# Bringing each block's gate and up biases by DMA, and adding them with two-row products

## What is computed

```python
logits = (xf @ w_router + b_router)
top_v, top_e = lax.top_k(logits, TOP_K)          # 4 of 32 experts
...
def expert_block(args):
    xe, e = args
    gu = xe @ w_gu[e] + b_gu[e]                  # 1024 -> 2048, gate and up interleaved
    gate = jnp.minimum(gu[..., 0::2], SWIGLU_LIMIT)
    up = jnp.clip(gu[..., 1::2], -SWIGLU_LIMIT, SWIGLU_LIMIT)
    act = (up + 1.0) * (gate * jax.nn.sigmoid(gate * SWIGLU_ALPHA))
    return act @ w_dn[e] + b_dn[e]
```

## Time and profile before

| what | us |
|---|---|
| median of 3 runs | 1533.24 |
| lowest and highest | 1531.03 and 1533.29 |
| the profiled execution's own time | 1530.54 |
| its span, first to last instruction | 1528.2 |

### The profile page before, as it was taken

The page is one execution under the profiler, slowest core; times in us unless marked ns, Lnnn a source line. Parts: engine busy times, 40 slices in busy tenths (PEclk is TensorE's granted clock), DMA queues, the critical chain, the costliest instruction groups (busy, mean ns, idle before and its releaser), DMA issues.

```text
span 1528.2 us, 20819 instructions
## 1 busy us (share of the span) xinstructions
PE 1453.2 (95%) x6962; PEld 1184.8 (78%) x6962; DVE 1304.7 (85%) x1231; ACT 1016.8 (67%) x903; POOL 203.9 (13%) x149
## 2 busy tenths in 40 slices
PE   5999989778999999999999999999999999999994
PEld 5776867666888888888888888888888888888882
DVE  5348554768999999999999999999999999999998
ACT  5334444336777777777777777777777777777771
POOL 0000000021111112211111111112211112111100
PEclk9999999878999999999999999999999999999997
DMA  9311030349999999999999999999999999999994
GB/s 353 113 68 56 33 138 15 120 170 378 360 372 367 361 376 360 371 373 369 377 382 372 376 368 366 362 377 365 371 372 375 378 371 373 379 366 361 366 375 166
DMA packets 98157, 471.77 MB, mean 309 GB/s; under 512 B 12649, under 2 KB 12690, under 8 KB 63826
## 3 DMA queue, kind: packets, MB, share of 16 engines
q1 hardware_dynamic: 87682, 451.72, 75.9%
q0 software_dynamic: 10448, 19.70, 3.6%
HBM read 467.70 MB, written 21.50 MB: 320 GB/s over the span
## 4 chain that ended last, share of the span: by engine, by line
PE 89%; DVE 7%; DMA 1%; issue 1%; ACT 1%; SPq 0%; DVEq 0%; ACTq 0%; POOLq 0%
PE gu_bank L1246 17%; PE gu_bank L1247 17%; PE gu_bank L1248 17%; PE turn_bank L1246 8%; PE turn_bank L1248 8%; PE turn_bank L1247 8%; PE bank L1494 2%; PE bank L1501 2%; DVE w_lo L828 2%; PE bank L1246 2%; PE bank L1248 1%; PE bank L1247 1%; PE gu_bank L1486 1%; PE bank L1418 1%; PE gu_bank L1364 1%
## 5 line engine op out<-in xcount | busy, mean ns | idle before, releaser
L828 DVE TENSOR_TENSOR w_lo<-raw,w_hi 128x2048 fp32r<-128x2048 f32 x411 | 931.9, 2288 | 113.3 <-ACT w_hi L578 107.7
L578 ACT ACTIVATE w_hi<-raw 128x2048 fp32r<-128x2048 f32 x411 | 784.8, 1921 | 231.1 <-PE gu_bank L1248 187.0
L1246 PE MATMUL gu_bank<-w_hi,turned 128*128 128x512 f32 (+1 forms) x1096 | 430.5, 393 | 8.5 <-DVE turned L1129 8.2
L1247 PE MATMUL gu_bank<-w_lo,turned 128*128 128x512 f32 (+1 forms) x1096 | 427.1, 390 | 0.0
L1248 PE MATMUL gu_bank<-w_hi,turned 128*128 128x512 f32 (+1 forms) x1096 | 426.8, 389 | 0.0
L1246 PEld LDWEIGHTS gu_bank<-w_hi,turned 128*128 128x128 f32 x1096 | 207.2, 189 | 51.0 <-issue 7.1
L1248 PEld LDWEIGHTS gu_bank<-w_hi,turned 128*128 128x128 f32 x1096 | 207.2, 189 | 42.8
L1247 PEld LDWEIGHTS gu_bank<-w_lo,turned 128*128 128x128 f32 x1096 | 207.4, 189 | 41.3
L1246 PE MATMUL turn_bank<-w_hi,turned 128*128 128x512 f32 (+1 forms) x544 | 213.4, 392 | 0.0
L1248 PE MATMUL turn_bank<-w_hi,turned 128*128 128x512 f32 (+1 forms) x544 | 210.4, 387 | 0.0
L1247 PE MATMUL turn_bank<-w_lo,turned 128*128 128x512 f32 (+1 forms) x544 | 210.3, 387 | 0.0
(11 more groups left out here) (265 smaller groups left out, 1303.7 us busy)
## 6 DMA issues: line engine op xcount, KB each, us to landing
raw<-in_w_gate_up_dram SPq DMA_DIRECT2D x264, 1024.0 KB, 7.7
raw<-in_w_down_dram SPq DMA_DIRECT2D x132, 1024.0 KB, 9.7
raw<-in_w_in_dram SPq DMA_DIRECT2D x10, 1024.0 KB, 7.7
raw<-in_w_out_dram SPq DMA_DIRECT2D x4, 1024.0 KB, 5.5
raw<-expert_rows SPq DMA_DIRECT2D x4, 1024.0 KB, 6.2
raw<-in_w_mem_kv_dram SPq DMA_DIRECT2D x2, 1024.0 KB, 8.9
arena<-in_x_dram SPq DMA_DIRECT2D x1, 2048.0 KB, 14.6
arena<-in_position_tables_dram SPq DMA_DIRECT2D x1, 2048.0 KB, 19.5
```

Source lines behind the costliest of these rows:

```text
L578: a.activation(home, raw_ap, ACT.Copy).then_inc(hi_ready, 1)
L828: v.tensor_tensor(home[1], raw_ap, home[0].bitcast(F32), ALU.subtract).then_inc(lo_ready, 1)
L1246: pe.matmul(bank, a[0], b[0], start=first, stop=False)
L1247: pe.matmul(bank, a[0], b[1], start=False, stop=False)
```

## The change

All of the split biases are written once from `bias` to a tensor in memory, `split_biases` (512 KB), by Pool. For each block Pool then reads the block's expert's rows back: four transfers of 2 rows (high and low) by 512 numbers, each to two partitions of `bias_now`, at partitions 0, 32, 64 and 96. `gu_bias` adds them with four products of 2 rows by a tile of ones, `ones_r`, one product in each group of 32 partitions, and waits for the four transfers instead of for `pick`. The expert's number is read by Pool (`value_load`) from `exp_i`. DVE makes `ones_r` once and no longer makes `pick`.

```diff
+    bias_dram = nc.dram_tensor("split_biases", (P, FF), F32).ap()
+    bias_rows = bias_dram.rearrange("(g i e) (h n) -> i e h g n", g=2, i=2, h=2)
...
-        pick = R[:, 7 * D:7 * D + P]
+        ones_r = R[:, 7 * D:7 * D + P]
+        bias_now = R[:, 5 * D:5 * D + 512]
...
+            def bias_of(e):
+
+                for c in range(4):
+                    pool.dma_start(bias_now[c * E:c * E + 2, :].unsqueeze(1),
+                                   bias_rows[:, e, c // 2, c % 2, :]).then_inc(bias_now_in, 16)
+
+            pool.wait_ge(bias_ready, 2)
+            pool.dma_start(bias_dram, bias).then_inc(bias_saved, 16)
+            pool.wait_ge(bias_saved, 16)
+            bias_of(slice(0, 1))
             pool.tensor_copy(idx_scatter, y_row_i[:, bass.ds(loops, 1)]).then_inc(idx_ready, 1)
...
+            def bias_of_block(b):
+
+                bias_of(bass.ds(pool.value_load(exp_i[0:1, bass.ds(b, 1)], min_val=0, max_val=E - 1), 1))
+
             with pool.Fori(1, loops) as b:
                 pool.wait_ge(xtp_done, b + 1)
                 gather(bass.ds(b + 1, 1), b * 2 + 1)
+                bias_of_block(b)
                 scatter(b - 1, b * 2 + 2)
+            pool.wait_ge(xtp_done, loops + 1)
+            bias_of_block(loops)
             scatter(loops - 1, loops * 2 + 1)
...
                 link(v.tensor_copy(bias, bias_in))
+                v.tensor_copy(ones_r, ones).then_inc(ones_ready, 1)
...
-            def choose(into, ready, column):
-
-                v.tensor_scalar(into, cst[:, C_ROWMOD:C_ROWMOD + 1].to_broadcast([P, P]), exp_f[:, column], None,
-                                ALU.is_equal).then_inc(ready, 1)
...
-            def gu_bias(n_pick):
-
-                pe.wait_ge(pick_ready, n_pick)
+            def gu_bias(n_in):
+
+                pe.wait_ge(bias_now_in, n_in)
                 for c in range(4):
-                    rows = slice(c % 2 * 2 * E, (c % 2 + 1) * 2 * E)
-                    ins = pe.matmul(psum[c], pick[rows, :], bias[rows, c // 2 * 512:(c // 2 + 1) * 512],
-                                    start=False, stop=True)
+                    rows = slice(c * E, c * E + 2)
+                    ins = pe.matmul(psum[c], ones_r[rows, :], bias_now[rows, :], start=False, stop=True)
                 ins.then_inc(gu_done, 1)
...
-            pe.wait_ge(bias_ready, 2)
-            gu_bias(1)
+            pe.wait_ge(ones_ready, 1)
+            gu_bias(64)
...
-                gu_bias(b + 1)
+                gu_bias(b * 64 + 64)
```

More of the change, by code:

```diff
@@ L289, in hymba_layer @@
         atp_done, ahi_ready, alo_ready = sem("atp_done"), sem("ahi_ready"), sem("alo_ready")
-        pick_ready = sem("pick_ready")
+        ones_ready, bias_saved, bias_now_in = sem("ones_ready"), sem("bias_saved"), sem("bias_now_in")
         map_ready, map_in, map_out, part_in, part_added = (
@@ L1164, in _ @@
             number_blocks()
-            choose(pick, pick_ready, slice(0, 1))
             for i in range(4, GU):
@@ L1171, in _ @@
             clamp(1)
-            choose(pick, pick_ready, slice(1, 2))
             lo_m(GU + 2)
@@ L1186, in _ @@
                 clamp(b + 1)
-                choose(pick, pick_ready, bass.ds(b + 1, 1))
                 lo_m(GU + 11, b)
```

## The result

| | before | after |
|---|---|---|
| median, 5 runs each | 1533.29 us | 1543.09 us |
| lowest and highest | 1531.03 and 1535.58 | 1542.29 and 1545.75 |

The ratio is 1.0067, with a 95% interval of 1.0051 to 1.0083: slower by 9.8 us in the medians. Forecast were 5.7 us. The profiled execution of after took 1545.5 us, with a span of 1543.8.

The account below looks back on a forecast made before the run. The prediction took PE, full in the loop, to bound the kernel. It added 16.4 us at the start and took off 10.7 in the loop, +5.7 on 1533.24, for 1539 us, range 1531 to 1546.

Parts of the forecast that it names:

- What bounds the kernel: In the loop PE is busy 35.00 of 35 us without waits, so a microsecond off PE is one off the time.
- The write behind the loads: Ahead of the loop, the 512 KB write follows Pool's earlier loads in its queue, landing 15.7 us after its issue.
- The four reads: Ahead of the loop, after the write: the fourth read starts 1.5 us later and lands in 3.1, biases there at 363.4.
- The start: Ahead of block 1: PE waits for write and reads, starting at 370.0 instead of 353.67, +16.4 us once.
- the wait for `turn_x`: Sign at the start, between blocks 0 and 1: PE waits again about 6 us for L1129.
- The step saved on PE: Bias products in the loop: one step in place of two saves 0.335 us per block, -10.7 us over 32 blocks.
- The Trainium skill's factor: Bias products in the loop: four row-packed products at 3.07 times one after the other, saving 0.23 a block, 7.4 us in all.
- In the loop, hidden: Pool's reads for block 2 land at 408.2 to 414.0, before PE needs them at 414.58.
- Rival 1: At the start, the write doesn't queue and lands in 4.0 us: sum -6.1, 1527 us; chance 0.10.
- Rival 2: In the loop, biases come late in every block: at 10 us to the landing +15, 1554 us; chance 0.04.
- Rival 3: The four bias products don't run at once, nothing saved: +16.4, 1549.6 us; chance 0.06.

Follow-up runs that it names:

- block 0 the old way: The changed kernel, but block 0's biases are added as in the kernel before, blocks 1 to 32 the new way: 1524.8 us, ratio 0.9952 to the kernel before.

## Why the prediction was right, point by point

The forecast was 1539 us, slower, with 1531 to 1546 as its range; 1543.09 lies in it. The mechanism held, and one term was mis-sized.

- **What bounds the kernel.** Right: PE has no wait in the loop of after, and what was saved per block came off the time, as the kernel with block 0 the old way shows on its own.
- **The write behind the loads.** Right, and nearly to the number: 15.7 us from issue to landing forecast, 15.8 measured, with 3.7 us behind the slowest load where 3.0 were taken. The choice between a bound of 4.0 and one of 17.7 was made by asking what stood ahead of it in the same queue, and moving those loads took 7.1 us off. What this didn't foresee is the rest: even then it needs 8.75.
- **The four reads.** 1.5 us of issue and 3.1 to the last landing forecast, 1.55 and 2.62 measured. The reason given (a small read with nothing ahead of it in its queue) was luck in part: the weight loads had just run dry. A read that met other transfers took 5.36, and in the loop of after the reads take 6.0 at the median.
- **The start.** +16.4 us forecast (its own terms, 370.0 - 353.67, give 16.3), +16.9 measured. The forecast left out the 0.28 us between the end of `split_biases` and the write, as much again before the reads, and 0.14 before the products; the reads' 0.5 less paid for most of it. Of its signs one failed here: the wait for `turn_x` is 4.2 us, not about 6.
- **The step saved on PE.** Too large: 0.335 us a block taken, 0.224 measured, 10.7 against 7.2 us over 32 blocks. This is 3.5 of the 4.1 us by which the forecast was short. The other 0.5 are the start's. The step that failed is the reading of the earlier trace rows: the second pair stands 0.335 behind the first, and I took the distance for the price of a pair. But a lone pair takes 0.43 to the turning of the rows, a lone set of four 0.43 to 0.44, and a second pair or a second set costs 0.21 to 0.24 more. So 0.335 holds a part that the first set pays whatever follows, most likely its own weight load, which finds no product to hide behind (that it is the load wasn't tried by itself); the set taken away was worth about one step of the products around it, 0.23. The row was there: the products of 128 rows start 0.23 apart, and the second pair is at work beside the first's tail.
- **The Trainium skill's factor** ("TensorE: Matmul & The Clock Gate", Part 3, measured speedup: 3.07 for four packed products) gave 7.4 us for this term, an estimate, and the measured 7.2 stands by it rather than by mine. In part this is luck: the factor is for four products one after the other, and it was applied to the step of 0.335, which is not the price of one.
- **In the loop, hidden.** Right: the fourth read was issued at about 426.9 (425.27 + 2.10 less one issue of 0.5) and had until 437.2. The slowest of all reads in the loop landed 7.3 us after its issue, 3 us in time, and leaving the reads out changed nothing.
- **Rival 1** (the write doesn't queue) fell at the landing of 15.8. The Trainium skill ("DMA: Bandwidth & Descriptors", Anatomy of one DMA) gives 2.0 us plus bytes over 436 GB/s, by which this write would take an estimated 3.2 us: the traces don't agree, with 15.8 here, 8.75 without the loads ahead of it, and 4.0 for a write of this size in the quiet stretch. **Rival 2** (late in every block) fell with PE's empty list of waits. **Rival 3** (not at once) fell: four starts within 0.01 us, and 0.22 us a block gained.

## What to carry to other kernels

When data that a loop needs takes a detour through memory, look at its first use by itself: the detour was free for 32 blocks and cost 16.9 us for the one that had no work in front of it, and keeping the old path for that one block turned 10 us lost into 8 us gained. Before you price a transfer, ask what was issued on the same queue just before, and what else keeps the DMA engines busy: here the first was worth 7.1 of 15.8 us, and the write without it still took 8.75 against 4.0 in a quiet stretch. The distance between the starts of the first two members of a short series is not the price of a member: take it from a run with one member more or less (0.21 to 0.24 us here), or from the distance in steady flow (0.23).

## What the runs showed of the hardware that was not expected

- A set of products in different partition groups takes 0.43 us from its first product to the next products when it stands alone between products of 128 rows, whether it is two of 64 rows or four of 2 rows, and 0.21 to 0.24 for each further set.
- A read of 4 KB issued by Pool took 2.62 us where the weight loads had just run dry, 5.36 where weights and other loads of Pool were moving, and 6.0 at the median in the loop.
- The granted clock between 200 and 250 us was 0.97 in some traces and 0.86 in others, with nothing in that part changed. Each kernel has one trace, but the kernel before alone had a mean granted clock of 0.978 at about 1530.7 us and of 0.972 at about 1535.7: about 5 us of the time.
- After PE's wait at the start the granted clock was back at 1.00 after 6.0 us in before and after, and after 3.6 us with the loads moved, for a reason that no run shows.
